# Score tiles on three PSUM banks and two tiles ahead, maxima back on two banks, in an attention stage shared with paged decoding

## Chip, cores, metric

One core of one Trainium2 chip. The metric is the device time of one execution in microseconds (us). Before the change: median 3564.12 us of 3 runs (3557.31 to 3565.9).

## What is computed

One layer of a hybrid decoder (forgetting attention beside an RG-LRU branch, then a gated convolutional FFN), for one prompt of 2048 tokens with 16 meta tokens ahead of it, and for 8 samples of one token each that attend to 4096 cached positions in pages of 128. What the change touches is the attention of both:

```python
def forget_attend(q, cq, qpos, k, v, ck, kpos):
    s = jnp.einsum('bqhd,bkhd->bhqk', q, k).astype(jnp.float32) * ATT_SCALE
    s = s + jnp.swapaxes(cq, 1, 2)[:, :, :, None] - jnp.swapaxes(ck, 1, 2)[:, :, None, :]
    s = jnp.where(kpos[None, :] <= qpos[:, None], s, -jnp.inf)
    p = jax.nn.softmax(s, axis=-1)
    return jnp.einsum('bhqk,bkhd->bqhd', p.astype(v.dtype), v)
```

There are 8 heads of 64, and 8 samples, each with 32 pages of keys and 32 of values; a page of all heads is 128 x 512 numbers, 256 KB.

## The kernel before

Every engine runs its own program in order, and they meet on semaphores. Phases follow each other: projections, the attention ("heads", some 930 us of the span, from 768 to 1700 us), then output projection and FFN, where TensorE multiplies without a break. The change is in the heads alone.

**One turn per head.** Turn i computes prompt head i, prepares the row maxima of head i + 1, finishes the decoding of sample i (weights times cached values), and computes the scores of sample i + 1. The tables `PLANS` hang each of these small steps on one of the 51 score tiles (`TILES`) of a turn. All engines walk through the same tiles and do, at tile t, those steps of `plan[t]` that are theirs. There is a plan for the first turn, one for turns 1 to 6, and one for the last.

**Prompt scores.** Tile t has 128 keys by up to 416 queries. `scores(t)` (L2224, L2226, at the diagonal L2229) writes it to a PSUM bank, ScalarE takes the exponential into one of three buffers PT (L1235), `values(t)` (L2240) multiplies by the values. Before, there are two banks for scores, 0 and 1, and TensorE runs `scores(t + 1)`, `values(t)`, then `plan[t]`.

**Maxima of the next head.** They need the scores of head i + 1 in the other orientation, in 45 pieces p. TensorE computes piece p (`max_piece`, L2163, at the diagonal L2167 as well) at tile 5 + 36 p // 44, VectorE takes its row maximum (`piece_max`, L1685) at the same tile of its own walk. The pieces rotate over banks 2, 3 and 6, so TensorE may begin piece p when VectorE has reduced piece p - 3.

**Decoding.** SyncE walks over 16 groups g of two pages: value pages g of sample i (V below), then key pages g of sample i + 1 (K). Value buffers are four groups deep: V of group g waits (L555) until TensorE has used group g - 4, which it does in `pages(m)` (L2264), m = 0 to 7, two groups at a time. So V 8 waits for `pages(2)`, V 10 for `pages(3)`, V 14 for `pages(5)`. In turns 1 to 6 `pages(2)` hangs on tile 19, `pages(5)` on tile 36. K of a group is issued behind V of the same group. After K 11 SyncE issues the staging of head i + 2 (`fetch_head`, L508 to L511, four transfers of 520 KB each). GpSimd multiplies the landed keys by the query (L830), VectorE sums the products (`page_scores`, L1734). In the plan of turns 1 to 6 the sum of group 6 hangs on tile 17, of group 12 on tile 34, of group 13 on 35, 14 on 37, 15 on 38.

The pieces that matter below, with their tiles in turns 1 to 6: p14 on 16, p15 on 17, p16 and p17 on 18, p18 on 19; p36 on 34, p37 on 35, p38 and p39 on 36, p40 on 37. In a tile's list pieces stand ahead of page sums and of `pages`:

```python
        for p in range(len(PIECES)):
            plan[5 + 36 * p // 44].append(("piece", p))
    ...
            if g % 2:
                plan[5 + (37 if last else 43) * g // 15].append(("pages", g // 2))
            if not last:
                plan[8 + 3 * g // 2 if g < 8 else 28 + 3 * (g - 8) // 2].append(("scores", 16 + g))
```

**End of a turn.** When the sum of group 15 is in, VectorE ends the scores of sample i + 1, GpSimd takes their maximum over partitions (L837), ScalarE the exponentials (L1173), between those of tiles; `pages(7)` on tile 48 closes sample i, and on its semaphore SyncE begins the next turn.

Of the kernel before, what the change touches and what calls it, by code (L numbers as in the profile page):

```python
# [17 lines left out]
ACT = mybir.ActivationFunctionType  # L18
# [24 lines left out]
LASTP = TPR - (NB - 1) * BW  # L43
PAGES = 32
DEN_W = 43
DVE_FIRST = 10
NPG = NS * PAGES
NIN = 21
# [73 lines left out]
TILES = score_tiles()  # L122
# [59 lines left out]
def build(nc, a, out):  # L182
    ctx = ExitStack()
    with ctx:
# [78 lines left out]
        PT = sb("PT", [P, 3, BW], F32, m2)  # L263
# [78 lines left out]
        PS = ctx.enter_context(nc.psum_tensor("PS", [P, 8, 512], F32))  # L342
# [67 lines left out]
        ex = sem("ex")  # L410
# [554 lines left out]
        def _(e):  # L965
# [108 lines left out]
            with e.Fori(0, 2) as i:  # L1074
# [7 lines left out]
                for u in range(2):  # L1082
                    c = 2 * i + u
                    n = 9 + 3 * c
# [18 lines left out]
                    for j in range(NB):  # L1103
# [11 lines left out]
                        if j == 0:  # L1115
# [4 lines left out]
                                     scale=sp[:, bass.ds(c, 1), 0]).then_inc(r_act, 1)  # L1120
                        e.activation(RA[:, cols(j)], RT[:, 1], ACT.Exp, bias=sp[:, bass.ds(c, 1), 6],
                                     scale=sp[:, bass.ds(c, 1), 6]).then_inc(r_act, 1)
# [107 lines left out]
            def act_head(i, u, plan):  # L1230
                for t, (j, kt, q0, n, kr) in enumerate(TILES):
                    e.wait_ge(sT, 51 * i + t + 1)
                    if t >= 3:
                        e.wait_ge(pv, 51 * i + t - 1)
                    e.activation(PT[0:kr, t % 3, 0:n], PS[0:kr, (u + t) % 2, 0:n], ACT.Exp, scale=0.125).then_inc(ex, 1)  # L1235
                    for what, n in plan[t - 1] if t else ():
                        if what == "row":
                            maxima_row(i + 1, 1 - u, n)
                        if what == "exps":
                            sample_exp(i + n, (u + n) % 2)  # L1240
                        h, v, blocks = (i, u, NB - 1) if n else (i - 1, 1 - u, NB)
                        if what == "evict":
                            evict(i, u, n)
                        if what == "evict last":
                            evict(i - 1, 1 - u, NB - 1)
                        if what == "row out":
                            row_out(h, v, blocks)
                        if what == "turned":
                            turned_out(h, blocks)
                        if what == "spread":  # L1250
                            spread(h, blocks)
                        if what == "store":
                            store_out(h, v, blocks)
# [205 lines left out]
        def _(e):  # L1459
# [125 lines left out]
            with e.Fori(0, 2) as i:  # L1585
                g_steps.start(i, 2 * 13)
                for u in range(2):
                    c = 2 * i + u
                    n = 9 + 3 * c
# [181 lines left out]
            def dve_head(i, u, plan):  # L1771
                def invert(i, rows, w):

                    e.wait_ge(rd_ld, 48 * i + 16)
                    e.reciprocal(RD[0:rows, 1, 0:w], RD[0:rows, 0, 0:w]).then_inc(rd, 1)

                def times(i, u, w):

                    e.wait_ge(rd_ld, 48 * i + 48)
                    e.tensor_tensor(AO[0:HD, u, 0:w], AO[0:HD, u, 0:w], rden[:, 0:w], ALU.mult).then_inc(rd, 1)  # L1780

                for t in range(len(TILES)):
                    for what, n in plan[t]:
                        v = (u + n) % 2
                        if what == "divide":
                            sample_divide(i - 1 + n)
                        if what == "weight sum":
                            sample_invert(i)
                        if what == "keep":
                            sample_keep(i - 1 + n)  # L1790
                        if what == "piece":
                            piece_max(i + 1, n, (2, 3, 6))
                        if what == "products":
                            if n < DVE_FIRST:
                                page_products(0, 0, n)
                        if what == "scores":
                            page_scores(i + n // 16, (u + n // 16) % 2, n % 16)
                        if what == "end":
                            scores_end(i + n, v)
                        if what == "less":  # L1800
                            scores_less(i + n, v)
                        if what == "sums":
                            sample_sums(i + n, v)
                        if what == "invert":
                            invert(*((i, HD, 26) if n else (i - 1, 48, DEN_W)))
                        if what == "times":
                            times(*((i, u, (NB - 1) * BW) if n else (i - 1, 1 - u, TPR)))
# [225 lines left out]
        def _(e):  # L2033
# [75 lines left out]
            with e.Fori(0, 2) as i:  # L2109
                for u in range(2):  # L2110
                    c = 2 * i + u
                    n = 9 + 3 * c
# [102 lines left out]
            def pe_head(i, u, plan):  # L2215
                def scores(t):
                    j, kt, q0, n, kr = TILES[t]
                    if t == 0:
                        e.wait_ge(na, 5 * i + 5)
                        e.wait_ge(prep, 7 * i + 7)  # L2220
                    e.wait_ge(ex, 51 * i + t + 3)
                    o = PS[0:kr, (u + t) % 2]
                    ks, qs = slice(kt * P, kt * P + kr), slice(q0, q0 + n)
                    e.matmul(o[:, 0:n], KA[0:HD + 4, u, ks], QA[0:HD + 4, u, qs], start=True, stop=False)  # L2224
                    d = min(n, kt * P + P - q0)
                    mm = e.matmul(o[:, 0:n], KB[:, u, ks], QB[:, u, qs], start=False, stop=d <= 0)  # L2226
                    if d > 0:
                        m = q0 - kt * P
                        mm = e.matmul(o[:, 0:d], identB[0:kr, 0:kr], maskK[0:kr, m:m + d], start=False, stop=True)  # L2229
                    mm.then_inc(sT, 1)  # L2230

                def values(t):
                    j, kt, q0, n, kr = TILES[t]
                    if kt == 0:
                        e.wait_ge(on, 5 * i + j + 4)
                        if j == 0:
                            e.wait_ge(va_ld[u], 16 * (i - u) + 32)
                    e.wait_ge(ex, 51 * i + t + 5)
                    o = q0 - j * BW
                    e.matmul(PS[0:HD + 1, 4 + (u + j) % 2, o:o + n], VA[0:kr, u, kt], PT[0:kr, t % 3, 0:n], start=(kt == 0),  # L2240
                             stop=t in ENDS).then_inc(pv, 1)

                def weight_sum():

                    e.wait_ge(dn, 2 * i + 2)
                    e.wait_ge(at_s, i + 1)
                    e.sem_inc(go, 1)
                    e.matmul(PS[:, 7, 0:1], dwide[:, u], onesF[:, 0:1], start=True, stop=True).then_inc(df, 1)

                def pages(g):  # L2250
                    if g == 0:
                        e.wait_ge(od_s, 2 * i + 2)
                        if isinstance(i, int) and i == 0:
                            e.wait_ge(c_att2, 4)
                    for b in (2 * g, 2 * g + 1):
                        e.wait_ge(vg_ld[b % 4], 32 * (4 * i + b // 4) + 32)
                    ends = g == PAGES // 4 - 1
                    if ends:
                        e.wait_ge(nw_ld, 48 * i + 48)
                        e.sem_inc(go, 1)  # L2260
                        e.matmul(PS[0:NH, 7, :], sn[0:1, u, :], vnew[:, u], start=False, stop=False)
                    for c in range(4):
                        page = 4 * g + c
                        mm = e.matmul(PS[32 * c:32 * c + 32, 7, :],  # L2264
                                      scw[:, u, page:page + 4, :].rearrange("p a h -> p (a h)"),
                                      Vpg[:, (page // 2) % 4, page % 2], start=(g == 0), stop=ends)
                        if c % 2:
                            mm.then_inc(vd, 1)

                scores(0)  # L2270
                for t in range(len(TILES)):
                    if t + 1 < len(TILES):
                        scores(t + 1)
                    values(t)
                    for what, n in plan[t]:
                        if what == "columns":
                            sample_columns(i - 1 + n)
                        if what == "piece":
                            max_piece(i + 1, 1 - u, n, (2, 3, 6))
                        if what == "row":  # L2280
                            maxima_rows(i + 1, n)
                        if what == "weight sum":
                            weight_sum()
                        if what == "pages":
                            pages(n)
# [221 lines left out]
```

## Time and profile before

| | |
|---|---|
| median of 3 runs | 3564.12 us |
| profiled execution | 3566.58 us |
| its span | 3564.8 us |
| TensorE (PE) busy | 3095.1 us, 87% of the span |
| VectorE (DVE) busy | 1425.6 us, 40% |
| ScalarE (ACT) busy | 742.4 us, 21% |
| GpSimd (POOL) busy | 1219.4 us, 34% |
| a turn of the heads, 1 to 6 | 113 to 120 us |

All times in the trace are microseconds from the start of the span. Busy time is that of engines alone; SyncE (SPq), which issues the transfers, does nothing but wait and issue, and its time shows only in the chain and in the timeline.

### The profile page before, as it was taken

Reading aid. Unit: us, or ns where it says so; the run is one execution under the profiler, and the core shown is the slowest. Engines: PE = TensorE matmul, PEld = TensorE weight load, DVE = VectorE, ACT = ScalarE, POOL = GpSimd, SP = SyncE. Lnnn points to the kernel's source line nnn. Section 1 sums busy time; section 2 is a strip of 40 time slices with the busy share of each in tenths; the row PEclk is TensorE's granted clock in tenths of the full one; section 3 lists DMA queues with packets and bytes.
Section 4 is the critical chain, followed back from the end, with each engine's and each line's share of the span. In section 5 each row is a group of like instructions: output and inputs, shape, how many; then the busy total and the mean of one; then the engine's idle time right before and its main releaser. Section 6 shows DMA issues by size and latency. Waiting matters only on the chain.

```text
span 3564.8 us, 47261 instructions
## 1 busy us (share of the span) xinstructions
PE 3095.1 (87%) x15376; PEld 2681.3 (75%) x15376; DVE 1425.6 (40%) x1880; ACT 742.4 (21%) x1250; POOL 1219.4 (34%) x582
## 2 busy tenths in 40 slices
PE   4898989675677777789689999999999997999998
PEld 4898879542343434444689999999999997999998
DVE  4213333365445443541621655555555553121220
ACT  5100222221222222223300100000000002333332
POOL 1011101135445534560566422222222222444443
PEclk8899989866788887889899999999999998999999
DMA  6211444445757665674434311111111114554553
GB/s 186 81 69 60 103 99 95 88 109 152 217 160 210 174 182 168 188 206 119 140 106 152 100 46 47 43 47 48 48 48 48 48 36 140 170 177 156 188 188 104
DMA packets 253574, 422.40 MB, mean 118 GB/s; under 512 B 49265, under 2 KB 156954, under 8 KB 248906
## 3 DMA queue, kind: packets, MB, share of 16 engines
q1 hardware_dynamic: 167986, 322.58, 30.3%
q10 hardware_dynamic: 85152, 97.07, 9.1%
q8 instruction: 59, 0.97, 0.1%
q0 software_dynamic: 288, 1.05, 0.1%
q14 instruction: 89, 0.73, 0.1%
HBM read 337.21 MB, written 83.46 MB: 118 GB/s over the span
## 4 chain that ended last, share of the span: by engine, by line
PE 64%; SPq 9%; issue 8%; DMA 7%; DVE 6%; POOL 4%; ACT 2%; ACTq 0%; DVEq 0%; POOLq 0%
PE PS L2340 31%; PE PS L2063 12%; SPq L536 4%; PE PS L2426 4%; PE PS L2428 4%; PE PS L2427 4%; SPq L537 3%; DMA Kpg<-in_cache_k 2%; PE PS L2240 2%; POOL prod L830 2%; PE PS L2331 1%; DMA GR<-gT 1%; POOL DL L961 1%; PE PS L2264 1%; PE PS L2044 1%
## 5 line engine op out<-in xcount | busy, mean ns | idle before, releaser
L2340 PE MATMUL PS<-MH,VH 128*128 128x416 f32 x2000 | 708.4, 354 | 10.8 <-POOL VL L904 8.3
L2340 PE MATMUL PS<-ML,VH 128*128 128x416 f32 x2000 | 702.1, 351 | 0.0
L2340 PE MATMUL PS<-MH,VL 128*128 128x416 f32 x2000 | 701.9, 351 | 0.0
L2163 PE MATMUL PS<-KA,QA 68*128 68x512 f32 (+3 forms) x360 | 225.4, 647 | 194.3 <-DVE MP L1685 157.3
L2340 PEld LDWEIGHTS PS<-MH,VH 128*128 128x128 f32 x2000 | 376.1, 188 | 17.8 <-issue 12.4
L830 POOL TENSOR_TENSOR prod<-Kpg,qb 128x1024 f32<-128x1024 f32 x118 | 284.6, 2412 | 295.1 <-DMA Kpg<-in_cache_k 215.8
L2240 PE MATMUL PS<-PT,VA 128*65 128x416 f32 (+16 forms) x816 | 355.0, 521 | 30.9 <-ACT PT L1235 30.4
L2340 PEld LDWEIGHTS PS<-ML,VH 128*128 128x128 f32 x2000 | 377.2, 189 | 4.2 <-issue 0.8
L961 POOL TENSOR_TENSOR DL<-DR,DH 128x1408 fp32r<-128x1408 f32 x80 | 259.3, 3241 | 353.5 <-ACT DH L1381 353.4
L2340 PEld LDWEIGHTS PS<-MH,VL 128*128 128x128 f32 x2000 | 376.4, 188 | 4.8
L898 POOL TENSOR_TENSOR VR<-VR,gains 128x1024 f32<-128x1024 f32 x52 | 99.1, 1905 | 793.5 <-PE PS L2340 695.5
L2426 PE MATMUL PS<-GH,DH 128*128 128x416 f32 x880 | 320.3, 364 | 48.2 <-POOL DL L961 29.2
L2063 PE MATMUL PS<-XH,WH 128*128 128x416 f32 x840 | 306.9, 365 | 19.7 <-issue 11.6
L1235 ACT ACTIVATE PT<-PS 128x416 f32<-128x416 f32 (+16 forms) x408 | 186.6, 459 | 616.2 <-PE PS L2226 408.2
L2427 PE MATMUL PS<-GL,DH 128*128 128x416 f32 x880 | 313.6, 356 | 0.0
L2428 PE MATMUL PS<-GH,DL 128*128 128x416 f32 x880 | 313.5, 356 | 0.0
L2063 PE MATMUL PS<-XH,WL 128*128 128x416 f32 x840 | 296.9, 353 | 0.0
L2163 PEld LDWEIGHTS PS<-KA,QA 68*128 68x128 f32 (+1 forms) x360 | 75.9, 212 | 293.8 <-DVE MP L1685 216.9
L2063 PE MATMUL PS<-XL,WH 128*128 128x416 f32 x840 | 296.2, 353 | 0.0
L1685 DVE TENSOR_REDUCE MP<-PS 128x1 f32<-128x512 f32 (+3 forms) x360 | 206.4, 600 | 103.7 <-PE PS L2163 52.2
L1734 DVE TENSOR_REDUCE scw<-prod 128x16 f32<-128x1024 f32 x128 | 155.7, 1216 | 221.4 <-POOL prod L830 221.0
L1347 ACT ACTIVATE GC<-GC 128x416 f32<-128x416 f32 x110 | 60.8, 552 | 824.9 <-DVE GC L1941 745.2
(263 smaller groups left out, 4586.8 us busy)
## 6 DMA issues: line engine op xcount, KB each, us to landing
Kpg<-in_cache_k SPq DMA_DIRECT2D x256, 256.0 KB, 3.0
Vpg<-in_cache_v SPq DMA_DIRECT2D x256, 256.0 KB, 3.0
DR<-in_w_down SPq DMA_DIRECT2D x80, 704.0 KB, 4.1
gT<-GO ACTq DMA_DIRECT2D x110, 208.0 KB, 1.9
GR<-gT SPq DMA_DIRECT2D x55, 416.0 KB, 4.9
VR<-in_w_up SPq DMA_DIRECT2D x44, 512.0 KB, 3.5
WR<-in_w_stream SPq DMA_DIRECT2D x21, 512.0 KB, 3.5
Qst<-qT SPq DMA_DIRECT2D x16, 520.0 KB
```

Source lines behind the costliest of these rows:

```text
L830: e.tensor_tensor(prod[:, g % 4], Kpg[:, g % 4], qb[:, v].unsqueeze(1).to_broadcast([P, 2, DATT]), ALU.mult).then_inc(kpp, 1)
L961: e.tensor_tensor(DL[:, h], DR[:, h], DH[:, h].bitcast(F32), ALU.subtract).then_inc(d_lo, 1)
L1235: e.activation(PT[0:kr, t % 3, 0:n], PS[0:kr, (u + t) % 2, 0:n], ACT.Exp, scale=0.125).then_inc(ex, 1)
L1685: e.tensor_reduce(MP[0:rows, qt, pc:pc + 1], PS[0:rows, banks[p % len(banks)], 0:n], AX.X, ALU.max).then_inc(mx, 1)
L1734: e.tensor_reduce(sc[:, v, 2 * g:2 * g + 2, :], p.rearrange("p b (h d) -> p b h d", d=HD), AX.X, ALU.add)\
L2063: mm = e.matmul(PS[:, j, 0:BW], w[:, u, k], x[:, k, cols(j)], start=(k == 0 and q == 0), stop=(k == KC - 1 and q == 2))
L2163: mm = e.matmul(o[:, 0:n], QA[0:HD + 4, v, qt * P:qt * P + rows], KA[0:HD + 4, v, k0:k0 + n], start=True, stop=not diag)
L2240: e.matmul(PS[0:HD + 1, 4 + (u + j) % 2, o:o + n], VA[0:kr, u, kt], PT[0:kr, t % 3, 0:n], start=(kt == 0), stop=t in ENDS).then_inc(pv, 1)
L2340: mm = e.matmul(PS[:, j, 0:BW], w[:, u, k], x[:, k, cols(j)], start=(k == 0 and q == 0), stop=(k == KC - 1 and q == 2))
L2426: e.matmul(PS[:, v, 0:BW], DH[:, h, k], GH[:, r, m], start=(kk == 0), stop=False)
L2427: e.matmul(PS[:, v, 0:BW], DH[:, h, k], GL[:, r, m], start=False, stop=False)
L2428: e.matmul(PS[:, v, 0:BW], DL[:, h, k], GH[:, r, m], start=False, stop=(kk == FC - 1))\
```

## The change

Scores use banks 0, 1 and 6 in turn, by t mod 3, and `scores(t)` waits for the exponential of tile t - 3 instead of t - 2. TensorE issues `scores(0)` and `scores(1)` ahead of the loop and `scores(t + 2)` ahead of `values(t)`. Bank 6 is taken from the pieces: they rotate over banks 2 and 3, and piece p waits for the reduction of piece p - 2.

```diff
+SCORE_BANKS = (0, 1, 6)
...
-                    e.activation(PT[0:kr, t % 3, 0:n], PS[0:kr, (u + t) % 2, 0:n], ACT.Exp, scale=0.125).then_inc(ex, 1)
+                    e.activation(PT[0:kr, t % 3, 0:n], PS[0:kr, SCORE_BANKS[t % 3], 0:n], ACT.Exp, scale=0.125).then_inc(ex, 1)
...
-                            piece_max(i + 1, n, (2, 3, 6))
+                            piece_max(i + 1, n, (2, 3))
...
-                    e.wait_ge(ex, 51 * i + t + 3)
-                    o = PS[0:kr, (u + t) % 2]
+                    e.wait_ge(ex, 51 * i + t + 2)
+                    o = PS[0:kr, SCORE_BANKS[t % 3]]
...
                 scores(0)
+                scores(1)
                 for t in range(len(TILES)):
-                    if t + 1 < len(TILES):
-                        scores(t + 1)
+                    if t + 2 < len(TILES):
+                        scores(t + 2)
                     values(t)
                     for what, n in plan[t]:
...
                         if what == "piece":
-                            max_piece(i + 1, 1 - u, n, (2, 3, 6))
+                            max_piece(i + 1, 1 - u, n, (2, 3))
```

How TensorE's order moves, at tiles 46 and 47 of a middle turn, where the score tiles have sizes of their own (KA, QA are the augmented keys and queries, KB, QB the other pair, PT the exponentials, NM the negated maxima; L2179 is a step of `plan[t]`). Before, the scores of tile 48 (272 queries) stand ahead of the values of tile 47:

```order
L2179 MATMUL PS<-identF,NM 66x128 [waits na]
L2179 MATMUL PS<-identF,NM 66x128 x3
L2224 MATMUL PS<-QA,KA 128x272 [waits ex]
L2226 MATMUL PS<-QB,KB 128x272
L2229 MATMUL PS<-maskK,identB 128x128
L2238 REGISTER_ALU
L2240 MATMUL PS<-PT,VA 65x400 [waits ex]
```

Of the change, the same place, one source line further down: the scores of tile 49 (144 queries) stand there.

```order
L2180 MATMUL PS<-identF,NM 66x128 [waits na]
L2180 MATMUL PS<-identF,NM 66x128 x3
L2225 MATMUL PS<-QA,KA 128x144 [waits ex]
L2227 MATMUL PS<-QB,KB 128x144
L2230 MATMUL PS<-maskK,identB 128x128
L2239 REGISTER_ALU
L2241 MATMUL PS<-PT,VA 65x400 [waits ex]
```

So each values product has one more score tile ahead of it. Pieces and page products keep their places. This is tile 36 of the change on TensorE, pieces p38 and p39 and then `pages(5)` (Vpg are value pages, scw the sample's weights); only the count behind "waits mx" is another:

```order
L2241 MATMUL PS<-PT,VA 65x400 [waits ex]
L2160 REGISTER_ALU
L2164 MATMUL PS<-KA,QA 128x512 [waits mx]
L2160 REGISTER_ALU
L2164 MATMUL PS<-KA,QA 128x512 [waits mx]
L2168 MATMUL PS<-maskQ,identB 128x128
L2265 MATMUL PS<-Vpg,scw 32x512 [waits vg_ld3,vg_ld2]
L2265 MATMUL PS<-Vpg,scw 32x512 x3
```

And this is VectorE there, the same before and after: the reduction of p36, the sum of page group 12, the reduction of p37, the sum of group 13, the reduction of p38.

```order
L1685 TENSOR_REDUCE MP<-PS 128x1 [waits mm_mx]
L1733 REGISTER_ALU
L1734 TENSOR_REDUCE scw<-prod 128x16 [waits kpp]
L1684 REGISTER_ALU
L1685 TENSOR_REDUCE MP<-PS 128x1 [waits mm_mx]
L1733 REGISTER_ALU
L1734 TENSOR_REDUCE scw<-prod 128x16 [waits kpp]
L1684 REGISTER_ALU
L1685 TENSOR_REDUCE MP<-PS 128x1 [waits mm_mx]
```

What the change moves there is none of these rows but the reduction that lets TensorE's p39 begin: p36 before (ahead of the sum of group 12), p37 after (behind it).

## Rows read from the trace of the kernel before

**Rows 1.** The page: TensorE's share of the span; busy us, instructions

```profile
PE 3095.1 (87%) x15376; PEld 2681.3 (75%) x15376; DVE 1425.6 (40%) x1880; ACT 742.4 (21%) x1250; POOL 1219.4 (34%) x582
```

**Rows 2.** Waits of TensorE, 765 to 1700: total us, times, longest

```profile
PE PS L2163 <- DVE MP L1685: 152.7, 47, 9.9
PE PS L2240 <- ACT PT L1235: 30.4, 14, 12.1
```

**Rows 3.** The chain that ended last, 1115 to 1245, by line

```profile
by line: issue 25.9%; SPq L536 23.8%; SPq L537 19.4%; DMA Kpg<-in_cache_k 5.8%; POOL prod L830 3.6%; PE PS L2264 3.0%; SPq L523 2.4%; PE PS L2240 2.1%; PE PS L2261 1.2%; DVE MP L1685 1.2%; PE PS L2163 1.1%; SPq L508 1.0%; SPq L510 0.9%; SPq
```

**Rows 4.** Waits of SyncE's queue, 765 to 1700

```profile
SPq L555 <- PE PS L2264: 104.2, 21, 23.7
```

**Rows 5.** Timeline of TensorE, last turn: start us, us, engine, line, operation

```profile
1690.02 0.35 PE L2226 MATMUL PS<-QB,KB 128*128 128x400 f32 x1
...
1691.06 0.34 PE L2226 MATMUL PS<-QB,KB 128*128 128x400 f32 x1
```

**Rows 6.** Timeline of VectorE, turn 2, tiles 34 and 35

```profile
1145.19 1.22 DVE L1734 TENSOR_REDUCE scw<-prod 128x16 f32<-128x1024 f32 x1 [12.01 <-POOL prod L830]
1146.33 0.68 DVE L1685 TENSOR_REDUCE MP<-PS 128x1 f32<-128x512 f32 x1
```

**Rows 7.** Timeline of SyncE (K 12) and of GpSimd, turn 2

```profile
1131.88 1.50 SPq L537 DMA_DIRECT2D Kpg<-in_cache_k  x2
...
1142.82 2.34 POOL L830 TENSOR_TENSOR prod<-Kpg,qb 128x1024 f32<-128x1024 f32 x1 [11.95 <-DMA Kpg<-in_cache_k]
```

**Rows 8.** Timeline of TensorE, turn 2: p38 and p39, pages(5), p40

```profile
1132.64 1.10 PE L2163 MATMUL PS<-KA,QA 68*128 68x512 f32 x2 [1.29 <-DVE MP L1685]
...
1133.75 1.94 PE L2264 MATMUL PS<-Vpg,scw 128*32 128x512 f32 x8
...
1147.06 0.63 PE L2163 MATMUL PS<-KA,QA 68*32 68x512 f32 x1 [9.43 <-DVE MP L1685]
```

**Rows 9.** Timeline of SyncE: V 14 of turns 1, 2, 5 and 6

```profile
1022.33 1.51 SPq L537 DMA_DIRECT2D Vpg<-in_cache_v  x2
...
1138.97 1.44 SPq L537 DMA_DIRECT2D Vpg<-in_cache_v  x2
...
1484.97 1.46 SPq L537 DMA_DIRECT2D Vpg<-in_cache_v  x2
...
1596.31 1.44 SPq L537 DMA_DIRECT2D Vpg<-in_cache_v  x2
```

**Rows 10.** Timeline of TensorE: p40 of turns 1, 5 and 6

```profile
1028.78 0.63 PE L2163 MATMUL PS<-KA,QA 68*32 68x512 f32 x1 [7.93 <-DVE MP L1685]
...
1492.50 0.63 PE L2163 MATMUL PS<-KA,QA 68*32 68x512 f32 x1 [8.27 <-DVE MP L1685]
...
1597.63 0.42 PE L2163 MATMUL PS<-KA,QA 68*32 68x512 f32 x1 [0.89 <-DVE MP L1685]
```

**Rows 11.** Timeline of TensorE, turns 1 and 2: pages(2), and p18 ahead of it

```profile
986.59 1.94 PE L2264 MATMUL PS<-Vpg,scw 128*32 128x512 f32 x8
...
1101.63 0.93 PE L2163 MATMUL PS<-KA,QA 68*128 68x512 f32 x1
1102.49 1.94 PE L2264 MATMUL PS<-Vpg,scw 128*32 128x512 f32 x8
```

**Rows 12.** Timeline of SyncE (V 8) and of VectorE (group 6), turns 2, 1, 2

```profile
1105.23 1.42 SPq L537 DMA_DIRECT2D Vpg<-in_cache_v  x2
...
984.70 1.20 DVE L1734 TENSOR_REDUCE scw<-prod 128x16 f32<-128x1024 f32 x1
...
1102.13 1.22 DVE L1734 TENSOR_REDUCE scw<-prod 128x16 f32<-128x1024 f32 x1 [1.45 <-POOL prod L830]
```

**Rows 13.** Timeline, end of turn 2: sum of group 15, values of tile 48

```profile
1153.03 1.22 DVE L1734 TENSOR_REDUCE scw<-prod 128x16 f32<-128x1024 f32 x1 [0.60 <-POOL prod L830]
...
1167.04 0.67 PE L2240 MATMUL PS<-PT,VA 128*65 128x272 f32 x2 [2.59 <-ACT PT L1235]
```

**Rows 14.** The page: the exponentials; mean ns of one before the last bar

```profile
L1235 ACT ACTIVATE PT<-PS 128x416 f32<-128x416 f32 (+16 forms) x408 | 186.6, 459 | 616.2 <-PE PS L2226 408.2
```

## The prediction

> **What bounds the kernel now.** I read the page first: TensorE is busy 87% of the span [rows 1], so its idle time is what a change of its order can win. Its waits in the heads say who makes it idle: 152.7 us before max pieces, released by VectorE's row maxima; 30.4 us before values products, released by the exponentials [rows 2]. So the wait that the third score bank can shorten is the second, and the wait that the lost piece bank can lengthen is the first, five times as large.
>
> Then I asked who really sets a turn's length, by the chain that ended last over a stretch of one turn. It hardly runs over TensorE: two lines of SyncE, which load a page number and issue its transfer, hold 43% of it, key landings and GpSimd's products follow, and TensorE's page products have 3% [rows 3]. That 3% is the important part. SyncE's queue stands 104.2 us in all waiting for TensorE's page products to free a value buffer [rows 4], and as K of a group is issued behind V of the same group, a late page product makes the keys late, and with them GpSimd, VectorE's sums and the end of the turn. A turn ends with the sum of group 15; 14.0 us behind it come the values of tile 48 and `pages(7)` [rows 13], which let SyncE begin the next turn. So a microsecond lost by SyncE is lost in full, and a microsecond lost by TensorE is lost only if it stands before a page product that SyncE waits for.
>
> **The change part by part.** *No instruction is added or removed.* The same matmuls, exponentials and reductions run; banks and wait counts differ.
>
> *Scores two tiles ahead.* Worth what TensorE waits for exponentials. In a steady tile nothing is to be had: from one score matmul to the next are 1691.06 - 1690.02 = 1.04 us, without idle time [rows 5], while an exponential takes 0.46 us on average [rows 14] and already has the previous values product and the next scores to hide under. Of the 30.4 us, one wait alone is 12.1 us [rows 2], and the wait at the end of a turn (2.59 us) has the same cause [rows 13]: it is before tile 48, where ScalarE itself stands at the sample's exponentials, for which VectorE and GpSimd are late. Scores that lie ready do not shorten that. I take 0; bounds 0 and the full 30.4 us. What it costs: at a turn's start one more score tile stands ahead of the page products, about 0.35 us [rows 5], in turns where `pages(0)` is not waited for. 0 as well.
>
> *Pieces on two banks: pages(5).* This is the term. In turn 2 SyncE issues K 12 at 1131.88, the staging of a whole head is ahead of it in the transfers, and GpSimd gets it at 1142.82, after 11.95 us of waiting [rows 7]. So VectorE stands 12.01 us at the sum of group 12 (tile 34), until 1145.19, and reduces p37 only at 1146.33 [rows 6]. Where does TensorE stand meanwhile? With three banks p38 and p39 need the reductions of p35 and p36, both done before the stall: they run at 1132.64, `pages(5)` follows at 1133.75, and only p40, which needs p37, is held, until 1147.06 [rows 8]. V 14 is issued at 1138.97, later than `pages(5)` allows [rows 9]: nobody waits for it. With two banks **p39 needs p37**, and p39 stands ahead of `pages(5)`. So p39 starts when p40 starts now, 1147.06; a full piece soon behind a stall takes 0.86 us until the next matmul begins [rows 11]; I take 0.9 with its mask; from the start of such page products to the issue of the V behind them are 1105.23 - 1102.49 = 2.74 us [rows 11, 12]. V 14 moves to 1147.06 + 3.6 = 1150.7, that is by 11.7 us, and V 15, K 14 and K 15 with it. The same sum gives 1028.78 + 3.6 - 1022.33 = 10.1 us in turn 1 and 1492.50 + 3.6 - 1484.97 = 11.1 us in turn 5 [rows 9, 10]; turns 3 and 4 repeat the pattern. **Five turns at 11.0 us are 55 us.** Turn 6 stages no further head, p40 was held 0.89 us only, and the sum gives 1597.63 + 3.6 - 1596.31 = 4.9 us, rather 4, since behind so short a stall p40 took 0.42 us and not 0.63 [rows 9, 10]. Turn 0 has another plan, in which the last piece stands ahead of `pages(5)` and of the sum behind the long stall, and turn 7 has no pieces: 0. Together 59 us. Nothing covers this: SyncE has no other work, and behind K 15 the chain is bare.
>
> *The same at pages(2).* p18 on tile 19 stands ahead of `pages(2)`. Three banks: it needs p15 (tile 17, ahead of the sum of group 6). Two: it needs p16, which VectorE reduces behind that sum. In turn 2 the sum starts at 1102.13 [rows 12], lasts 1.14 us to the next reduction, that one 0.68 us [rows 6], p18 then 0.86: `pages(2)` starts at 1104.8 instead of 1102.49, 2.3 us later [rows 11]. Here SyncE was already waiting, so V 8 moves by the whole of it. Turn 1 gives 984.70 + 2.68 - 986.59 = 0.8 us [rows 11, 12]. Four turns are like turn 2, two like turn 1: 4 x 2.3 + 2 x 0.8 = 11 us. As K 12 moves with V 8, this adds to the term above.
>
> *The other pieces.* TensorE is held one piece earlier in each stall and has that tile's work left when VectorE lets it go. Before `pages(0)`, `pages(1)` and `pages(4)` SyncE is not waiting, and at the end of a turn TensorE has 2.59 us to spare [rows 13]. I take 0. Bounds: nothing, and a slow tile (twice the 1.04 us of a steady one [rows 5] and the piece's 0.86 us, about 3 us) once per turn, 20 us, with 12 us more if the slack at the turns' ends is used up too.
>
> Sum: 59 + 11 = 70 us on the profiled execution, whose own time of 3566.58 is 2.5 us above the median of the runs: 3564.1 + 70 = **3634 us, 2% slower**.
>
> **Rivals.**
> 1. *One tile per stall, no more.* If V 14 is late for another reason, or has more slack than its issue time shows, only the earlier holds count: about one tile of 1.3 to 3 us in six turns, 8 to 18 us, 3572 to 3582. Against it: V 14 is issued 8 us before p37 is reduced, in a program order that cannot bend. Chance 0.08.
> 2. *Faster.* TensorE's bubbles before the values products are closed by the extra score bank, at values of tile 48 and at the starts of query blocks, and the piece stalls, being VectorE's, stay as long as they are: 3564 - 30 = 3534 us. It decides if score tiles, not the sample's exponentials, are what ScalarE waits for at those places. For it: ScalarE waits for scores in most of its idle time [rows 14]. Against it: SyncE's chain does not pass there, and turns would end no sooner. The Trainium skill, "Perfetto Trace Analysis", sections Identifying the Most-Contended Engine and Optimization Strategy, would lead here: look for the gaps on the engine with the highest occupancy, and take a repeated gap as a sign of too few buffers. By that rule one gets 30 us or more; the chain [rows 3] speaks against applying it to TensorE. Chance 0.03.
> 3. *No change:* the time lost at `pages(5)` is got back because a later K 14 finds empty transfer queues and the next turn's start has slack. For it, nothing: K 15 lands into an empty queue now too. 3564 within 10 us. Chance 0.05.
>
> The forecast has the remaining 0.84. Within it: if piece and page product behind p39 run at their fast pace and a little is won at block starts, 3610; if the bounds of the other pieces hold, 3634 + 32 = 3666. The range reaches from 3605 to 3665 and leaves rivals 1 to 3 out. About 0.3% (11 us) is what a measurement of this kernel tells from no change. Faster by more: rival 2 and a little of 3, 0.04. Within: the rest of 3 and of 1, 0.06. Slower: 0.90.
>
> **What would show it.** The profile after should have, in turns 1 to 5, the long wait of some 10 us before p39 and not before p40, `pages(5)` behind it, SyncE's V 14 about 2.7 us behind `pages(5)` with a new wait of some 10 us, and turns longer by 10 to 14 us each; turn 6 longer by 6, turn 7 unchanged. The waits for the exponentials should stay near 30 us. The phases before and behind the heads should not move. The forecast is wrong if V 14 keeps its place, if p39 passes before the sum of group 12, or if the waits at tile 48 vanish and turns get shorter.

## The result, and the profile after

| | before | changed |
|---|---|---|
| median of 4 runs | 3562.88 us | 3618.69 us (3615.33 to 3621.22) |
| profiled execution, its span | 3566.58, 3564.8 us | 3621.05, 3619.3 us |

The ratio is 1.0158 [1.014, 1.0175]: 56 us slower, where 70 were forecast, inside the range.

The page of the changed kernel, its first lines and three of its costliest groups (busy, mean ns, then idle time before the group and who ended most of it):

```profile
span 3619.3 us, 47273 instructions
## 1 busy us (share of the span) xinstructions
PE 3113.5 (86%) x15376; PEld 2692.6 (74%) x15376; DVE 1430.7 (40%) x1880; ACT 740.4 (20%) x1250; POOL 1215.5 (34%) x582
...
L2164 PE MATMUL PS<-KA,QA 68*128 68x512 f32 (+3 forms) x360 | 232.1, 666 | 263.4 <-DVE MP L1686 223.6
...
L831 POOL TENSOR_TENSOR prod<-Kpg,qb 128x1024 f32<-128x1024 f32 x118 | 281.9, 2389 | 362.4 <-DMA Kpg<-in_cache_k 286.4
...
L2241 PE MATMUL PS<-PT,VA 128*65 128x416 f32 (+16 forms) x816 | 361.1, 529 | 15.5 <-ACT PT L1236 14.7
```

The waits in the heads, TensorE's and then SyncE's, of the changed kernel (us in total, times, longest):

```profile
PE PS L2164 <- DVE MP L1686: 219.1, 63, 11.8
PE PS L2241 <- ACT PT L1236: 14.7, 6, 10.9
```

```profile
SPq L556 <- PE PS L2265: 163.6, 28, 24.1
SPq L547 <- PE PS L2265: 109.9, 6, 21.8
```

They answer to [rows 2] and [rows 4]. The change does what it was built for: the waits for exponentials halve, from 30.4 to 14.7 us. But the waits for row maxima grow by 66 us (152.7 to 219.1), and, which is what counts, SyncE's waits for a value buffer by 59 us (104.2 to 163.6).

The forecast named one place, tile 36. This is turn 2 of the changed kernel there, TensorE's timeline without its scores and values:

```profile
1146.57 0.70 PE L2164 MATMUL PS<-KA,QA 68*128 68x512 f32 x1
1158.96 0.79 PE L2164 MATMUL PS<-KA,QA 68*128 68x512 f32 x1 [11.69 <-DVE MP L1686]
1159.55 0.33 PE L2168 MATMUL PS<-maskQ,identB 128*128 128x128 bf16 x1
1159.81 1.94 PE L2265 MATMUL PS<-Vpg,scw 128*32 128x512 f32 x8
...
1163.24 1.23 PE L2164 MATMUL PS<-KA,QA 68*32 68x512 f32 x1
```

VectorE and SyncE at the same place:

```profile
1157.08 1.22 DVE L1735 TENSOR_REDUCE scw<-prod 128x16 f32<-128x1024 f32 x1 [11.05 <-POOL prod L831]
1158.22 0.68 DVE L1686 TENSOR_REDUCE MP<-PS 128x1 f32<-128x512 f32 x1
```

```profile
1162.56 1.42 SPq L538 DMA_DIRECT2D Vpg<-in_cache_v  x2
```

p38 runs, p39 (the piece with a mask behind it) waits 11.69 us for the reduction of p37, which stands behind the sum of group 12; `pages(5)` starts 0.85 us after p39, V 14 is issued 2.75 us after `pages(5)`. Before, `pages(5)` passed ahead of the wait [rows 8]. V 14 follows `pages(5)` by 2.75 to 3.07 us in each of turns 1 to 5.

**Where the time went.** Each turn has three fixed marks on SyncE: the issues of V 0, V 8 and V 14. The lengths between them, changed minus before, account for the 54.6 us by which the heads grew:

| stretch | turn by turn | sum |
|---|---|---|
| up to V 0 of turn 1 | | +1.5 |
| V 0 to V 8 (turns 1 to 6) | -2.1, 2.5, 1.1, 3.3, 1.3, 4.3 | +10.5 |
| V 8 to V 14 (turns 1 to 6) | 12.3, 10.9, 10.8, 9.7, 10.7, 2.0 | +56.5 |
| V 14 to the next V 0 (turns 1 to 5) | -1.6, -1.1, 0.0, -1.1, -2.8 | -6.6 |
| V 14 of turn 6 to values of tile 48 in turn 7 | | -7.3 |

The +10.5 us of the second row scatter from turn to turn, because VectorE reaches the sum of group 6 at different times, and in turn 1 because SyncE waits for `pages(0)` there, which the prediction had ruled out: V 4 follows V 3 by 9.5 us before and 6.7 after, 4.5 to 5.4 in the other turns. Counted from the start of that sum they do not. `pages(2)` begins 0.36 us behind it in turns 2, 3, 4 and 6 of the kernel before and 1.9 us in turns 1 and 5; in the changed kernel it begins 2.6 to 2.75 us behind it in every turn. That is 2.2 to 2.4 us in four turns and 0.9 us in two, 10.8 us together. In turn 2 of the changed kernel the sum begins at 1112.54, and p18 waits for the reduction behind it:

```profile
1114.41 0.79 PE L2164 MATMUL PS<-KA,QA 68*128 68x512 f32 x1 [1.01 <-DVE MP L1686]
1115.14 1.94 PE L2265 MATMUL PS<-Vpg,scw 128*32 128x512 f32 x8
```

Behind the heads nothing moved. The windows of the stretch from the heads' end to the last instruction, before and then changed (length, busy time of PE, PEld, DVE, ACT, POOL, granted clock, DMA share, GB/s):

```profile
1701.00:3564.00 1863.00, 1759.28 (x9232) 1726.17 (x9232) 741.47 (x925) 339.80 (x455) 685.17 (x326) 0.97 0.30 99
```

```profile
1755.00:3619.00 1864.00, 1759.80 (x9232) 1726.67 (x9232) 742.79 (x925) 340.33 (x455) 683.61 (x326) 0.97 0.30 99
```

The last two rows of the table were not forecast. They lie at the turns' ends, where values of tile 48 wait for the sample's exponentials. At the end of turn 6, before:

```profile
1624.55 0.67 PE L2240 MATMUL PS<-PT,VA 128*65 128x272 f32 x2 [3.28 <-ACT PT L1235]
...
1635.68 0.95 PE L2291 MATMUL PS<-onesF,od 128*128 128x1 f32 x8
```

And of the changed kernel:

```profile
1685.91 0.67 PE L2241 MATMUL PS<-PT,VA 128*65 128x272 f32 x2
...
1692.94 0.95 PE L2293 MATMUL PS<-onesF,od 128*128 128x1 f32 x8
```

No wait any more, and the way to `sample_columns` of the next turn (L2291, L2293) takes 7.03 instead of 11.13 us. That is 4.1 of the last row's 7.3 us; 0.5 us lie ahead of it, and 2.6 us behind it, in turn 7. Windows over it, before and changed:

```profile
1624.00:1636.50 12.50, 11.95 (x47) 5.84 (x47) 1.26 (x3) 3.52 (x11) 0.00 (x0) 0.59 0.30 86
```

```profile
1685.50:1693.70 8.20, 8.07 (x52) 4.58 (x49) 1.04 (x2) 3.49 (x11) 0.00 (x0) 1.00 0.26 78
```

After a stop of 3.28 us TensorE's granted clock in this stretch was 0.59, near its lower level of 1.2 GHz; without the stop it was 1.00, that is 2.4 GHz. Some fifty matmuls that take 11.95 us there take 8.07 here. The other turns' ends, by the same two views: TensorE's wait before the values of tile 48 in us (a dash is none), and the granted clock of the 12 us from their start:

| turn | 1 | 2 | 3 | 4 | 5 | 6 |
|---|---|---|---|---|---|---|
| before, wait | 2.53 | 2.59 | 0.85 | 2.63 | 2.19 | 3.28 |
| before, clock | 0.57 | 0.57 | 1.00 | 0.53 | 0.58 | 0.57 |
| changed, wait | - | - | 0.53 | - | - | - |
| changed, clock | 1.00 | 0.68 | 1.00 | 0.86 | 1.00 | 1.00 |

The one turn that stopped for less than 1 us before, turn 3, had the full clock, and it is the one whose boundary won nothing. What shrinks is TensorE's last step of the turn: from the values of tile 48 to SyncE's first issue behind `pages(7)` are 4.25, 4.81, 2.90, 4.48 and 5.00 us in turns 1 to 5 before, and 2.90, 3.28, 2.90, 2.77 and 2.78 after, 6.8 us less in all, which covers the 6.6 us of the table.

The slow clock has not gone, it has moved. In the changed kernel TensorE is held at p43 and p44, which with two banks need the reductions of p41 and p42, behind the late sums of groups 14 and 15. Turn 2:

```profile
1173.52 0.63 PE L2164 MATMUL PS<-KA,QA 68*32 68x512 f32 x1 [5.47 <-DVE MP L1686]
1178.19 0.22 PE L2164 MATMUL PS<-KA,QA 68*32 68x16 f32 x1 [2.04 <-DVE MP L1686]
```

Before, p44 ran there without a wait:

```profile
1153.65 0.48 PE L2163 MATMUL PS<-KA,QA 68*32 68x16 f32 x1
```

From 1173 to 1185 the granted clock of the changed kernel was 0.51, and 1.00 again from 1185 until tile 48; before, it was 1.00 from 1153 to 1164. In this stretch the turn's end does not wait for TensorE: from the sum of group 15 to the sample's exponentials, by way of VectorE and GpSimd, are 12.2 to 13.1 us in every turn of both kernels. TensorE comes to tile 48 at 1190.9, 14.6 us behind the start of the sum of group 15 (1176.33); before, it was there at 1164.45, 11.4 us behind it [rows 13], and had to stop.

### The profile page after: what moved, and what is told of

Same layout as the page of the kernel before. It is cut to its first block, busy times and chain, and to the rows that moved or that the text cites. A ratio compares the mean times of both kernels' runs of the same rounds, so it can differ in the third digit from the quotient of the medians.

```text
span 3619.3 us, 47273 instructions
## 1 busy us (share of the span) xinstructions
PE 3113.5 (86%) x15376; PEld 2692.6 (74%) x15376; DVE 1430.7 (40%) x1880; ACT 740.4 (20%) x1250; POOL 1215.5 (34%) x582
## 4 chain that ended last, share of the span: by engine, by line
PE 64%; SPq 8%; DMA 8%; issue 7%; DVE 6%; POOL 5%; ACT 2%; ACTq 0%; DVEq 0%; POOLq 0%
PE PS L2342 31%; PE PS L2064 12%; SPq L537 4%; PE PS L2428 3%; PE PS L2430 3%; PE PS L2429 3%; SPq L538 3%; DMA Kpg<-in_cache_k 3%; PE PS L2241 2%; POOL prod L831 2%; DMA GR<-gT 2%; PE PS L2265 1%; PE PS L2333 1%; POOL DL L962 1%; PE PS L2164 1%
## 5 line engine op out<-in xcount | busy, mean ns | idle before, releaser
L2342 PE MATMUL PS<-MH,VH 128*128 128x416 f32 x2000 | 708.4, 354 | 11.8 <-POOL VL L905 8.3
L2241 PE MATMUL PS<-PT,VA 128*65 128x416 f32 (+16 forms) x816 | 361.1, 529 | 15.5 <-ACT PT L1236 14.7
L2064 PE MATMUL PS<-XH,WH 128*128 128x416 f32 x840 | 308.0, 367 | 19.9 <-issue 11.7
```

The source lines that it names most:

```text
L2064: mm = e.matmul(PS[:, j, 0:BW], w[:, u, k], x[:, k, cols(j)], start=(k == 0 and q == 0), stop=(k == KC - 1 and q == 2))
L2342: mm = e.matmul(PS[:, j, 0:BW], w[:, u, k], x[:, k, cols(j)], start=(k == 0 and q == 0), stop=(k == KC - 1 and q == 2))
```

## Experiments

The theory: a piece that waits for VectorE stands ahead of a page product that SyncE waits for. Rival A: the extra score tile ahead of each values product is the cost (or the gain at the boundaries). Rival B: it is the bank count by itself, in many small holds. Ratios are against the kernel before on the same chip.

### Banks alone

`e1_pieces_two`: the kernel before with pieces on two banks, scores as they were.

```diff
-                            piece_max(i + 1, n, (2, 3, 6))
+                            piece_max(i + 1, n, (2, 3))
...
-                            max_piece(i + 1, 1 - u, n, (2, 3, 6))
+                            max_piece(i + 1, 1 - u, n, (2, 3))
```

> The kernel before with only the bank part of the change: pieces on banks 2 and 3, scores on two banks and one tile ahead as before. My theory: pieces that wait for p - 2 put the wait before p39 and so before pages(5); the sum of its two terms was 70 us, the changed kernel lost 56, and the 13 us between lie in the turns' boundaries and in turn 7, where the score tiles lie ready. If they come from running two tiles ahead, this kernel loses what the changed one does and those 13 us as well: 3626 to 3640 us, turn 7 as long as before. Rival A: the 13 us have nothing to do with the scores (TensorE's clock is up at the turn's end because it no longer stands before tile 48): 3615 to 3622 us, as the changed kernel. Rival B: the loss comes from the scores, which stand ahead of page products: this kernel is within 10 us of 3563.

Measured 3625.72 us, 1.0185 [1.0152, 1.0217], between the two ranges, so that the time alone does not decide on rival A; the changed kernel has 1.0158, and the intervals overlap. V 14 is late against V 8 by 10.4, 9.8, 11.8, 7.7, 10.9 and 2.6 us in turns 1 to 6. The lost bank alone makes the whole loss. Most of the gain at the boundaries is here too, without any run-ahead: 5.8 of the 6.6 us in turns 1 to 5, and 4.8 of the 7.3 us behind V 14 of turn 6. TensorE's waits for exponentials and its window behind tile 48 of turn 6:

```profile
PE PS L2240 <- ACT PT L1235: 17.4, 14, 11.8
```

```profile
1684.40:1692.00 7.60, 7.29 (x48) 3.94 (x46) 0.75 (x1) 2.90 (x9) 0.00 (x0) 1.00 0.29 76
```

So most of the fall from 30.4 to 14.7 us is not the score bank's doing. TensorE waits at most 0.31 us before the values of tile 48 here, in every turn.

### Page products ahead of the pieces

`e2_pages_first`: the changed kernel, with `pages` at the front of each tile's list.

```diff
-    return plan
+    return [sorted(steps, key=lambda s: s[0] != "pages") for steps in plan]
```

> The changed kernel with one edit: in a tile's list the page products stand ahead of the pieces, so that pages(5) at tile 36 does not wait for p39 and pages(2) at tile 19 not for p18. Nothing else moves. My theory: both terms go, 54 us at V 14 and 10 us at V 8; what is left of the gain at the turns' boundaries stays: 3545 to 3562 us, V 14 issued as in the kernel before, the long wait still before p39 but with nobody behind it. Rival A (every piece stall costs a tile wherever it stands): 3590 us or more. Rival B (two banks slow VectorE and TensorE as a pair all along the turn): 3600 us or more.

Measured 3561.0 us, 1.0014 [0.9998, 1.0031]: banks and run-ahead are as in the change, and the loss is gone. TensorE's and SyncE's waits of this kernel in the heads:

```profile
PE PS L2164 <- DVE MP L1686: 173.6, 56, 11.8
PE PS L2241 <- ACT PT L1236: 21.1, 10, 11.5
```

```profile
SPq L556 <- PE PS L2265: 100.4, 19, 22.6
```

TensorE still stands 11.8 us at one piece and 21 us longer in all than before [rows 2]; it costs nothing, since SyncE is at 100.4 against 104.2 us [rows 4]. Rival B falls with it.

`e3_before_pages_first`: the same edit on the kernel before.

> The kernel before with the same edit, page products ahead of pieces. With three banks no long wait stands ahead of pages(5), so that term has nothing to win; pages(2), for which SyncE waits in each of six turns, is spared p18 (0.86 us): 4 to 8 us faster, 3554 to 3559 us. If the order of pieces and pages mattered beyond the waits named, it would be faster by 20 us or more. It is the base that e2 is compared with: the difference of the two is the change without its stalls.

A miss: 3560.17 us, 0.9999 [0.9982, 1.0017]. With three banks the pieces ahead of `pages` do no harm that can be measured. It is also the base for `e2_pages_first`: of the change 0.15% is left there, 5 us, inside the intervals.

`e6_pieces_two_pages_first`: two piece banks and the new order, scores one tile ahead.

> Pieces on two banks and page products ahead of pieces, scores as in the kernel before (two banks, one tile ahead). Against the changed kernel with page products first (3561 us) it lacks only the run of two tiles ahead. If that is worth anything by itself, this kernel is slower than that one: by 2 to 4 us if it helps at block starts and in turn 7 alone (3562 to 3566 us), by 10 us or more if it gave the 10 us by which the bank part alone was slower than the whole change. If the boundaries' gain has nothing to do with it: the same within 3 us.

Measured 3567.29 us, 1.0027 [1.0012, 1.0041], against 1.0014 [0.9998, 1.0031] of `e2_pages_first`, which runs two tiles ahead. In time the run-ahead may be worth up to some 5 us; the intervals overlap. The traces show a part of it: from the columns of turn 7 to its values of tile 48, the six traces with scores two tiles ahead are 1.9 to 2.6 us shorter than the kernel before, the six others with scores one tile ahead 0.2 to 1.0 us. So some 2 us in turn 7 belong to the run-ahead; whether there is more stays open.

### Which page product

`e9_after_pages5_first` and `e10_after_pages2_first`: the changed kernel, with the new order at tile 36 alone or at tile 19 alone, in turns 1 to 6.

```diff
+    if not first and not last:
+        plan[36].sort(key=lambda s: s[0] != "pages")
     return plan
```

> The changed kernel, with the page products ahead of the pieces at tile 36 alone (pages(5), turns 1 to 6). My two terms were 59 us for pages(5) and 11 us for pages(2); the changed kernel's trace has 56 and 10. This one keeps the second: V 14 as in the kernel before, V 8 some 2 us late a turn, 3565 to 3573 us. Rival (the stalls feed each other, so that one alone gives back most): within 4 us of before.

Measured 3573.53 us, 1.0024 [1.0008, 1.004], half a microsecond beyond the range: tile 36 gives back 1.34% of the 1.58%, 48 us. SyncE's and TensorE's waits:

```profile
SPq L558 <- PE PS L2267: 106.1, 20, 23.8
```

```profile
PE PS L2166 <- DVE MP L1688: 178.6, 62, 11.8
```

> The changed kernel, with the page products ahead of the pieces at tile 19 alone (pages(2)). It keeps the large term: 3600 to 3612 us, V 14 still some 10 us late against V 8. Rival (TensorE, freed at tile 19, gets to p39 before VectorE stalls): 3590 us or less.

Measured 3623.86 us, 1.0171 [1.0146, 1.0197]. That tile 19 leaves the large term alone is confirmed; that it wins 7 to 19 us is not, the time does not differ from the changed kernel's. In the trace the V 8 steps do shrink, from 10.5 to 1.7 us in sum (with a scatter of -5.9 to 4.4), but the part behind the heads is 5.9 us longer in this profile, and that part differs by 0 to 6 us between profiles of kernels that are alike there. Counted from the start of the sum of group 6, `pages(2)` gives back 6.7 of its 10.8 us only: the pieces of tile 18 still stand ahead of it and are held 2.6 to 5.0 us in every turn. The small term is seen in the trace and not resolved in the time.

### The same loss with three banks

`e11_before_pages5_tile37`: the kernel before, banks untouched; `pages(5)` goes one tile later, behind p40.

```diff
+    if not first and not last:
+        plan[36].remove(("pages", 5))
+        plan[37].append(("pages", 5))
     return plan
```

> The kernel before, three piece banks and two score banks untouched; only pages(5) of turns 1 to 6 moves from tile 36 behind tile 37's piece p40. By my theory the number of banks matters only through which piece stands ahead of pages(5): p40 waits for p37 with three banks as p39 does with two. So this kernel must show the same loss at V 14, five turns of 10 to 12 us, 3608 to 3622 us, with V 8 in place. If two banks cost something of their own (TensorE and VectorE out of step), it stays below 3590 us.

Measured 3620.61 us, 1.0165 [1.0133, 1.0196]. TensorE's timeline in turn 2 (without scores and values), and SyncE's V 14:

```profile
1137.83 1.10 PE L2166 MATMUL PS<-KA,QA 68*128 68x512 f32 x2
1138.77 0.23 PE L2170 MATMUL PS<-maskQ,identB 128*128 128x128 bf16 x1
1150.26 0.63 PE L2166 MATMUL PS<-KA,QA 68*32 68x512 f32 x1 [10.16 <-DVE MP L1688]
1150.83 1.94 PE L2267 MATMUL PS<-Vpg,scw 128*32 128x512 f32 x8
```

```profile
1153.57 1.42 SPq L540 DMA_DIRECT2D Vpg<-in_cache_v  x2
```

p38 and p39 pass at once as they did before, p40 waits, and `pages(5)` behind it is as late as with two banks: the same loss from moving one step by one tile. The steps from V 8 to V 14 grow by 58.3 us in the six turns, those to V 8 by none (-1.8). This is the cleanest evidence for the theory.

It also says where the boundary gain comes from. `pages(5)` is late here too, but the stops before tile 48 are still there (2.62, 2.59, 0.80, 2.50, 2.55, 2.69 us; clock 0.72, 0.56, 1.00, 0.50, 0.72, 0.57), and behind V 14 of turn 6 only 1.6 us are won instead of 7.3. In turns 1 to 5 a part of the gain is here all the same, 3.6 of the 6.6 us. With three banks TensorE is held at p44 (5.3 to 6.4 us), which needs p41, but not by the sum of group 15. With two banks it is held by that sum too (1.6 to 3.0 us at p44 in every turn of the changed kernel and of `e1_pieces_two`), and comes to tile 48 too late to stop. Two banks alone do not bring this about: `e9_after_pages5_first` and `e6_pieces_two_pages_first` have them, with V 14 in time, and stop for 0.8 to 3.5 us before tile 48, behind waits of 0 to 1.6 us at p44.

### The stall's source

VectorE stands at the sum of group 12 because K 12 lands late, behind the staging [rows 7]. `e4_fetch_late` (the changed kernel) and `e5_before_fetch_late` (the kernel before) issue the staging after the last keys.

```diff
-        if more > 1 and g == 11:
+        if more > 1 and g == 15:
```

> The changed kernel with one edit: SyncE issues the staging of head i + 2 behind K 15 and not behind K 11, so that K 12 does not queue behind 2 MB. My theory: the stall at the sum of group 12 (some 11 us in turns 0 to 5) goes, and with it the cause that made pages(5) late. V 14 then waits as in turn 6, 2 to 4 us. Against the changed kernel the five turns lose 54 us less 10 to 20: 3565 to 3590 us, if the staging still lands in time for GpSimd's preparation. SyncE's own issue time is unchanged. Rival: the keys are not late because of the staging but because of SyncE's pace of issue, and the stall before group 12 stays at 8 us or more: 3610 us or more. If the staging becomes late for the next turn instead, a wait of GpSimd before L810 of several us a turn shows, and the time is above 3590.

Measured 3573.04 us, 1.0045 [1.0029, 1.0062], within the range. Waits of SyncE:

```profile
SPq L556 <- PE PS L2265: 126.5, 25, 22.6
```

The long stall is gone, but the last piece before `pages(5)` still waits for a sum, 2.2 us in turn 2 and 1.2 to 3.2 us in all six. What that costs shows only against the kernel before with the same edit, which comes next.

> The kernel before with the staging of head i + 2 issued behind K 15. The stall at the sum of group 12 goes, but in this kernel pages(5) and V 14 never waited for it. What is won is SyncE's issue time of the four transfers, 2.6 us a turn ahead of K 12 to K 15, if the turn's end is what the chain says: 6 turns x 2.6 = 15 us at most, 3545 to 3555 us. Rival: the staging lands late for the next turn's preparation and gives it back: 3559 to 3575 us. With the changed kernel so edited at 3573 us this gives what the change costs where group 12 does not stall.

Measured 3543.64 us, 0.9955 [0.994, 0.9971]: **faster than both kernels**, and just below the range. The steps from V 8 to V 14 shrink by 15.3 us in the six turns, those to V 8 by 5.1. K 12 of turn 2, from SyncE's issue to GpSimd's product and VectorE's sum:

```profile
1120.78 1.51 SPq L537 DMA_DIRECT2D Kpg<-in_cache_k  x2
```

```profile
1125.23 2.37 POOL L830 TENSOR_TENSOR prod<-Kpg,qb 128x1024 f32<-128x1024 f32 x1 [2.24 <-DMA Kpg<-in_cache_k]
```

```profile
1127.63 1.22 DVE L1734 TENSOR_REDUCE scw<-prod 128x16 f32<-128x1024 f32 x1 [2.33 <-POOL prod L830]
```

From issue to use are 4.5 us, against 10.9 before; VectorE's stall falls from 12.01 [rows 6] to 2.33 us.

This is the base for `e4_fetch_late`, and the change costs 0.9% there, 1.0045 against 0.9955, some 32 us. SyncE's wait for value buffers says the same; here it is, against the 126.5 us above:

```profile
SPq L555 <- PE PS L2264: 94.5, 20, 22.0
```

So by the ratios the late landing of K 12 accounts for some 24 of the 56 us. The other 32 us are still there with the staging out of the way: between the two traces, the steps from V 8 to V 14 differ by 23.2 us and those from V 0 to V 8 by 13.3 us, and some 5 us are won back behind V 14 of turn 6.

### Both edits

`e7_after_both` and `e8_before_both` have late staging and page products first, on the changed kernel and on the one before.

> The changed kernel with page products ahead of pieces and the staging behind K 15. Each edit by itself took away most of the 56 us; both remove the wait before p39 and the stall that feeds it. If the late staging is worth the 2.6 us of issue time a turn, 3545 to 3555 us, ahead of both kernels; if it is neutral by itself, 3558 to 3564 us; if it makes the next turn's preparation late, as its 3573 us may say, 3565 us or more.

> The kernel before with the same two edits. Base for the last one: the difference of the two is the change where neither its stall nor the staging is in the way, and I expect it within 5 us of it, 3545 to 3562 us.

Measured 3553.16 us, 0.9979 [0.9966, 0.9993], within the range, and 3542.11 us, 0.9954 [0.9936, 0.9972], just below it, the best time of all and level with `e5_before_fetch_late`. Of the 32 us that the change costs with late staging, the order of the steps takes away most: the changed banks are 0.25% behind by the ratios, some 9 us where I expected 5 at most, with intervals that just overlap. I did not trace the cause of the rest; it stays open.

## Why the prediction was right, point by point

- **The place.** TensorE's idle time mattered only ahead of a page product. Right: the waits for exponentials fell by 16 us without a gain in the turns' body, and `e2_pages_first` lost no time with 21 us more of waits for maxima than before.
- **pages(5), 59 us.** Measured 56.5: five turns at 9.7 to 12.3 instead of 10.1 to 11.7, turn 6 with 2.0 instead of 4. `e9_after_pages5_first` gives back 48 us of it in the time, and `e11_before_pages5_tile37` makes the same loss out of the order alone.
- **pages(2), 11 us.** 10.5 in the trace at V 8, where it scatters from -2.1 to 4.3 turn by turn; counted from the sum of group 6, 10.8, with 2.2 to 2.4 us in four turns and 0.9 in two, as forecast. In the time it could not be resolved.
- **Scores two tiles ahead, 0.** Right within 5 us; the traces show some 2 us of gain in turn 7.
- **The step that failed: "The other pieces. I take 0", with bounds of 0 and +32 us.** The bound lay on the wrong side. I let the held work at most use up the 2.59 us of slack at a turn's end. It did use it up, and by that TensorE came to tile 48 with no stop; in four of the five turns whose ends had been slow the clock there rose to 0.86 or 1.00, and the boundary got shorter: -6.6 us in turns 1 to 5 and -7.3 behind them, 14 us that the sum of 70 lacks. The sum with them is 56. Of the 7.3 us, 4.1 lie between tile 48 and the columns, and 2.6 in turn 7, where they go with the run-ahead and not with the held work. With three piece banks and the same lateness of `pages(5)` the stops stayed, and 3.6 and 1.6 us were won instead of 6.6 and 7.3 (`e11_before_pages5_tile37`); why a part was won there in spite of the stops was not traced.
- **The range.** Its lower end, 3610 and less, was reckoned from a faster piece and page product behind p39 and a little at block starts. The time came out lower than 3634 for another reason: that term was 56.5 of 59, and the turns' ends gave the rest.
- **"Waits for exponentials stay near 30", "turn 7 unchanged".** Both wrong, for this same reason, and in turn 7 for the run-ahead as well. From V 0 to V 0, turns 1 to 5 grew by 8.7, 12.4, 11.9, 12.0 and 9.2 us, where I had 10 to 14.
- **The rivals.** 1 asked for more slack at V 14: there are 2.5 us in turn 2 (1138.97 against 1133.75 + 2.74 [rows 8, 9]), and they were in the sum. 2 took TensorE's bubbles as the bound; its only merit is the boundary gain, which came with two banks and no score bank (`e1_pieces_two`). 3 is excluded by the interval.

The Trainium skill, "Perfetto Trace Analysis", section Optimization Strategy, takes a bubble that repeats on the engine that should be saturated as a possible lack of buffers. Here the piece stall before `pages(5)`, 9.0 to 11.8 us, repeats in five turns. With the number of banks unchanged it left that place by order (`e2_pages_first`), and shrank to 1.2 to 3.2 us by an earlier landing (`e4_fetch_late`).

## What to carry over

Count a PSUM bank not by the idle time it makes or removes, but by which instruction then stands behind a wait, and what other queue waits for that instruction: here 12 us of standing was free ahead of one step and cost 11 us per turn ahead of the next. Put the instruction that another engine's queue waits for ahead of those that may be held, and bulk transfers for later behind the small ones that someone waits for now. And when a delay removes a stop elsewhere, look for what the clock gives back.

## What the runs showed of the hardware

- In the kernel before, the granted clock of the 12 us behind a stop of 2.2 to 3.3 us at the end of a turn was 0.53 to 0.58, and 1.00 behind one of 0.85 us and, in turns 1, 5 and 6 after the change, behind none (table above). At the end of turn 6 that was 4 us for one small stop. Behind stops of 2.5 to 2.7 us in `e11_before_pages5_tile37` it was 0.50 to 0.72. In turns 2 and 4 of the changed kernel the clock was 0.68 and 0.86 without a stop there; what lowered it I did not trace.
- VectorE's scaling of 64 x 2064 numbers with two inputs in SBUF and GpSimd's product of 128 x 1024 hinder one another, and either may be the one that pays. Before, turn 2, VectorE's and GpSimd's timelines:

```profile
1097.60 2.29 DVE L1780 TENSOR_TENSOR AO<-AO,rden 64x2064 f32<-64x2064 f32 x1
```

```profile
1097.73 4.37 POOL L830 TENSOR_TENSOR prod<-Kpg,qb 128x1024 f32<-128x1024 f32 x1 [1.30 <-DVE scw L1734]
```

  In `e2_pages_first`, the same turn, where GpSimd begins 0.18 us sooner than VectorE instead of 0.13 us later:

```profile
1092.18 4.32 DVE L1781 TENSOR_TENSOR AO<-AO,rden 64x2064 f32<-64x2064 f32 x1
```

```profile
1092.00 2.34 POOL L831 TENSOR_TENSOR prod<-Kpg,qb 128x1024 f32<-128x1024 f32 x1 [0.99 <-DMA Kpg<-in_cache_k]
```

  The two pairs differ in who came first; the other then takes 2 us longer. The more they overlap, the more it pays: in turn 4 before, GpSimd begins 1.13 us behind VectorE and takes 3.37 us, in turn 5 VectorE begins 1.00 us behind GpSimd and takes 3.51. The sum that lets p18 pass is near, so the V 8 steps scatter by a few microseconds either way. The Trainium skill, "GPSIMD Engine Reference", section Key points, states that GpSimd shares its SBUF interfaces with VectorE instructions that have two SBUF inputs; the trace agrees, and shows that the one that begins second pays.
- SyncE needs 2.33 to 2.43 us from one pair of pages to the next when it waits for nothing (V 12 at 1118.36, K 12 at 1120.78, V 13 at 1123.12 in turn 2 of `e5_before_fetch_late`; 2.27 us in turn 0 of the kernel before and some 2.5 in its turn 1), so a delay of its queue is not made up by issuing faster.
